# Two output column groups computed together with Strassen's method on half of the contraction

## The reference

```python
h = rmsnorm(x, norm_g)
q_a, k_a, v_a, g_a, u_p, g_p, q_m, g_m = split(h @ w_in)
y_a = moba_attention(q_a, k_a, v_a) * silu(g_a)                    # 8 heads x 128: 1024 wide
y_p = multiscale_pool(u_p, w_pool, pool_scale) * silu(g_p)         # 512 wide
y_m = memory_attention(q_m, *split(rmsnorm(mem) @ w_mem_kv)) * silu(g_m)   # 512 wide
y = concatenate([y_a, y_p, y_m]) @ w_out                           # (256 x 2048) @ (2048 x 2048)
return rmsnorm(x + y, final_norm_g)
```

## Time and profile before

| what | value |
|---|---|
| median of 3 runs | 437.32 us (437.22 to 437.8) |
| the profiled execution | 437.52 us |
| its span, first to last instruction | 435.4 us |
| mean granted TensorE clock | 0.997 of full speed |
| TensorE busy | 426.9 us (98%) |
| VectorE busy | 272.0 us (62%) |
| ScalarE busy | 223.1 us (51%) |
| POOL busy | 26.5 us (6%) |

### The profile page before, as it was taken

How to read it: one execution, slowest core, us unless ns; L and a number is a source line. 1 busy time by engine, 2 the same in 40 slices (tenths; PEclk the granted TensorE clock), 3 DMA queues, 4 the chain that set the end, 5 groups by cost and what they waited for, 6 DMA issues and landing times.

```text
span 435.4 us, 6073 instructions
## 1 busy us (share of the span) xinstructions
PE 426.9 (98%) x2276; PEld 367.7 (84%) x2276; DVE 272.0 (62%) x299; ACT 223.1 (51%) x303; POOL 26.5 (6%) x48
## 2 busy tenths in 40 slices
PE   9999999999999999999999999999999999999993
PEld 8888888888888888888988888888899888888882
DVE  4875865545464676746557677967668574648522
ACT  6864784743443435546544545455565545357311
POOL 1000000000000020000020200001000202120200
PEclk9999999999999999999999999999999999999998
DMA  8999959655556545542626556454645497756022
GB/s 284 403 401 411 402 202 383 188 186 191 183 184 190 193 159 176 177 139 100 213 98 199 188 190 192 152 192 172 215 145 191 137 401 237 213 174 193 0 98 97
DMA packets 25658, 89.78 MB, mean 206 GB/s; under 512 B 2976, under 2 KB 3232, under 8 KB 24736
## 3 DMA queue, kind: packets, MB, share of 16 engines
q1 hardware_dynamic: 24048, 81.16, 54.5%
q10 hardware_dynamic: 1584, 8.26, 4.8%
HBM read 87.31 MB, written 2.10 MB: 205 GB/s over the span
## 4 chain that ended last, share of the span: by engine, by line
PE 96%; issue 2%; DVE 0%; POOL 0%; ACT 0%; DVEq 0%; POOLq 0%
PE ps L405 35%; PE ps L408 17%; PE ps L421 11%; PE ps L423 11%; PE ps L422 11%; PE ps L386 3%; PE ps L393 1%; PE ps L503 1%; PE ps L458 1%; PE ps L494 1%; PE ps L473 1%; PE ps L495 0%; PE ps L457 0%; PE ps L469 0%; PE ps L563 0%
## 5 line engine op out<-in xcount | busy, mean ns | idle before, releaser
L770 DVE TENSOR_TENSOR w_lo<-w_raw,w_hi 128x1024 fp32r<-128x1024 f32 x137 | 173.9, 1282 | 107.8 <-ACT w_hi L580 107.5
L580 ACT ACTIVATE w_hi<-w_raw 128x1024 fp32r<-128x1024 f32 x137 | 143.6, 1058 | 124.6 <-PE ps L408 68.8
L405 PE MATMUL ps<-xT,w_hi 128*128 128x512 f32 x640 | 201.7, 396 | 0.0
L408 PEld LDWEIGHTS ps<-xT,w_lo 128*128 128x128 f32 x640 | 120.2, 188 | 28.4
L408 PE MATMUL ps<-xT,w_lo 128*128 128x256 f32 x640 | 125.8, 278 | 0.0
L405 PEld LDWEIGHTS ps<-xT,w_hi 128*128 128x128 f32 x640 | 97.8, 189 | 0.3
L421 PE MATMUL ps<-w_hi,yT 128*128 128x512 f32 x110 | 42.8, 389 | 0.0
L422 PE MATMUL ps<-w_lo,yT 128*128 128x512 f32 x110 | 42.8, 389 | 0.0
L423 PE MATMUL ps<-w_hi,yT 128*128 128x512 f32 x110 | 42.8, 389 | 0.0
L421 PE MATMUL ps<-w_hi,xT 128*128 128x512 f32 x64 | 25.4, 397 | 0.0
L423 PE MATMUL ps<-w_hi,xT 128*128 128x512 f32 x64 | 24.9, 390 | 0.0
(11 more groups left out here) (152 smaller groups left out, 399.6 us busy)
## 6 DMA issues: line engine op xcount, KB each, us to landing
w_raw<-in_w_in SPq DMA_DIRECT2D x96, 512.0 KB, 4.1
w_raw<-in_w_out SPq DMA_DIRECT2D x32, 512.0 KB, 4.2
w_raw<-in_w_mem_kv SPq DMA_DIRECT2D x13, 512.0 KB, 12.9
x_t_raw<-in_x_t SPq DMA_DIRECT2D x8, 256.0 KB, 13.3
rows<-in_x ACTq DMA_DIRECT2D x2, 1024.0 KB, 10.1
rows<-in_mem ACTq DMA_DIRECT2D x2, 1024.0 KB, 8.6
x_res<-in_x ACTq DMA_DIRECT2D x2, 1024.0 KB, 6.5
w_raw<-in_w_mem_kv SPq DMA_DIRECT2D x5, 256.0 KB, 5.4
```

Of the source, the lines that this page charges most:

```text
L405: pe.matmul(ps[:, bank0(g) + f, :], hi[:, t, f * P:(f + 1) * P], moving[:, kt], start=(kt == 0), stop=(kt == KT - 1), skip_group_check=True)
L408: m = pe.matmul(ps[:, bank0(g) + f, 0:S], lo[:, t, f * P:(f + 1) * P], moving[:, kt, 0], start=False, stop=(kt == KT - 1), skip_group_chec ...
L580: act.activation(halves_of(n)[0], w_raw[:, n % RAW], ACT.Copy).then_inc(hi_done, 1)
L770: dve.tensor_tensor(lo, w_raw[:, n % RAW], hi.bitcast(F32), ALU.subtract).then_inc(lo_done, 1)
```

## The change

Output groups 1 and 2 (`OUT1`, `OUT2`, 16 pieces) become one stretch of 22 units, 120 to 141. The contraction of branches 0 and 1 (8 of 16 tiles) is seen, for each branch, as a 2 x 2 block product: two halves of 128 tokens by two halves of the branch's four tiles, times those two halves by the two column groups. Seven block products with six matmuls each (`M1` to `M4`, `M6`, `N5`, `N7`) take the place of eight. The other two branches stay as they are (units `(OUT1, 4)` to `(OUT1, 7)` and the same of `OUT2`).

- Sums of weight blocks: f4 and f5 are each a plain load by SP and an adding DMA issued by POOL; f6 and f7 are sums by VectorE (`weight_sum`) at steps 118, 121, 124, 127. They are split into halves like a piece.
- Sums of `y` blocks: POOL makes four per branch right after VectorE has finished that branch (`block_sums`); ScalarE and VectorE split them in step 115.
- PSUM banks that hold a product needed in two results are copied once by ScalarE (four snapshots, `SNAPS`), and TensorE goes on adding into the bank. VectorE combines the snapshots with the residual (`combine`).
- SP's loop over the output groups is written out; it loads 14 pieces for the pair. The last group's split region shares memory with f5 to f7, so ScalarE waits for the low part of unit 141 before its first split there. `fg`, `squares` and some other buffers move in memory.

The diff, cut to its core:

```diff
-PIECES = GROUPS * PPG
+OUT1, OUT2 = OUT0 + 1, OUT0 + 2
+(M2, M3, M6, N5, M4, M1, N7) = range(GROUPS, GROUPS + 7)
+BRANCHES_MULTIPLIED = 2
+PAIR = OUT1 * PPG
+PAIR_UNITS = ((N5, 0), (M2, 0), (N5, 1), (M2, 1), (OUT1, 4), (M1, 0), (M3, 0), (OUT1, 5), (M1, 1), (M3, 1), (OUT1, 6),
+              (M4, 0), (M6, 0), (OUT1, 7), (M4, 1), (M6, 1), (OUT2, 4), (N7, 0), (OUT2, 5), (OUT2, 6), (N7, 1), (OUT2, 7))
+LAST_UNIT = PAIR + len(PAIR_UNITS)
+UNITS = LAST_UNIT + PPG
+LOADS = ((M2, 0), (M2, 1), (OUT1, 4), (M3, 0), (OUT1, 5), (M3, 1), (M6, 0), (M6, 1), (OUT1, 6), (OUT1, 7), (OUT2, 4),
+         (OUT2, 5), (OUT2, 6), (OUT2, 7)) + tuple((LAST, a) for a in range(PPG))
+F6, F7 = 1, 2
+SUM_STEPS = {OUT0 * PPG + 6: (F6, 0), PAIR + 1: (F6, 1), PAIR + 4: (F7, 0), PAIR + 7: (F7, 1)}
+SNAPS = {(M2, 1): 0, (N5, 1): 1, (M1, 1): 2, (M4, 1): 3}
+SNAPS_ORDER = (1, 0, 2, 3)
+OUT_BANK = {OUT0: 0, OUT1: 4, OUT2: 6, LAST: 0}
...
+        def unit(n):
+            if n < PAIR:
+                return divmod(n, PPG)
+            return PAIR_UNITS[n - PAIR] if n < LAST_UNIT else (LAST, n - LAST_UNIT)
+        def unit_of(g, a):
+            return LAST_UNIT + a if g == LAST else PAIR + PAIR_UNITS.index((g, a))
+        def piece_of(n):
+            if n < PAIR:
+                return n
+            return PAIR + LOADS.index(unit(n)) if unit(n) in LOADS else None
+        def slot(p):
+            return w_raw[:, p % RAW]
+        def whole_of(n):
+            if piece_of(n) is not None:
+                return slot(piece_of(n))
+            g, i = unit(n)
+            return f4[:, i] if g == N5 else f567[:, i, {M4: 0, M1: F6, N7: F7}[g]]
+        def sums_done(f, i):
+            return list(SUM_STEPS.values()).index((f, i)) + 1
...
-            if LAST * PPG <= n < LAST * PPG + SPLIT:
+            if LAST_UNIT <= n < LAST_UNIT + SPLIT:
                 return w_end[:, n % SPLIT, 0], w_end[:, n % SPLIT, 1]
             return w_hi[:, n % SPLIT], w_lo[:, n % SPLIT]
 
         def pieces_to_split(n):
 
 
-            ahead = n - (LAST * PPG - SPLIT)
+            ahead = n - (LAST_UNIT - SPLIT)
             if ahead < 0:
                 return range(n + SPLIT, n + SPLIT + 1)
-            return range(min(n + SPLIT + ahead, PIECES), min(n + SPLIT + ahead + 2, PIECES))
+            return range(min(n + SPLIT + ahead, UNITS), min(n + SPLIT + ahead + 2, UNITS))
...
-            with sp.Fori(0, GROUPS - OUT0) as g:
-                for a in range(PPG):
-                    sp.wait_ge(lo_done, g * PPG + ((OUT0 - 1) * PPG + a + 1))
-                    sp.dma_start(w_raw[:, a], out_w_dram[bass.ds(g, 1), a].rearrange("g p t c -> p (g t) c")
-                                 ).then_inc(landed[a], 16)
+            for a in range(PPG):
+                sp.wait_ge(lo_done, (OUT0 - 1) * PPG + a + 1)
+                sp.dma_start(w_raw[:, a], out_w_dram[0, a]).then_inc(landed[a], 16)
+            for r, (g, a) in enumerate(LOADS):
+                if r == 1:
+                    sp.wait_ge(probs_turned, 2 * len(JOBS))
+                    for i in range(BRANCHES_MULTIPLIED):
+                        sp.dma_start(f4[:, i], out_w_dram[OUT2 - OUT0, 2 * i]).then_inc(f4_landed[i], 16)
+                if r == 5:
+                    sp.wait_ge(piece_used, OUT0 * PPG)
+                    for i in range(BRANCHES_MULTIPLIED):
+                        sp.dma_start(f567[:, i, 0], out_w_dram[OUT1 - OUT0, 2 * i]).then_inc(f5_landed[i], 16)
+                if r < RAW:
+                    sp.wait_ge(lo_done, PAIR - RAW + r + 1)
+                else:
+                    past, i = LOADS[r - RAW]
+                    sp.wait_ge(lo_done, unit_of(past, i) + 1)
+                    if past == M6:
+                        sp.wait_ge(f67_done, sums_done(F6, i))
+                    if past == M3:
+                        sp.wait_ge(f67_done, sums_done(F7, i))
+                src = {M2: (OUT2, 2 * a), M3: (OUT2, 2 * a + 1), M6: (OUT1, 2 * a + 1)}.get(g, (g, a))
+                sp.dma_start(slot(PAIR + r), out_w_dram[src[0] - OUT0, src[1]]).then_inc(landed[(PAIR + r) % RAW], 16)
...
+            def block_sums(i):
+                s1, s2, s3, s4 = (s_raw[:, i, j] for j in range(4))
+                a11, a21 = gate[:, 0:TPP, 0:P], gate[:, 0:TPP, P:S]
+                a12, a22 = gate[:, TPP:NF, 0:P], gate[:, TPP:NF, P:S]
+                pool.wait_ge(y_ready, i + 1)
+                pool.tensor_tensor(s1, a21, a22, ALU.subtract).then_inc(s_step, 1)
+                pool.tensor_tensor(s3, a11, a21, ALU.subtract).then_inc(s_step, 1)
+                pool.wait_ge(s_step, 3 * i + 1)
+                pool.tensor_tensor(s2, s1, a11, ALU.subtract).then_inc(s_step, 1)
+                pool.wait_ge(s_step, 3 * i + 3)
+                pool.tensor_tensor(s4, a12, s2, ALU.add).then_inc(s_summed, 1)
             for i, g in enumerate(GATES):
+                if g == MEM_JOB:
+                    for k in range(BRANCHES_MULTIPLIED):
+                        pool.wait_ge(f4_landed[k], 16)
+                        pool.dma_start(f4[:, k], out_w_dram[OUT1 - OUT0, 2 * k], accum_op=ALU.add).then_inc(f4_summed[k], 16)
                 pool.wait_ge(gate_tanh, i + 1)
                 pool.wait_ge(att_ready, 2 * (i + 1))
                 pool.tensor_tensor(gate[:, :, :], gate[:, :, :], att[:, i % 2], ALU.mult).then_inc(gate_att, 1)
+                if i < BRANCHES_MULTIPLIED:
+                    block_sums(i)
+            for k in range(BRANCHES_MULTIPLIED):
+                pool.wait_ge(f5_landed[k], 16)
+                pool.dma_start(f567[:, k, 0], out_w_dram[OUT1 - OUT0, 2 * k + 1], accum_op=ALU.add).then_inc(f5_summed[k], 16)
...
+            def block_product(n):
+                hi, lo = halves_of(n)
+                g, i = unit(n)
+                first, second = slice(0, P), slice(P, S)
+                bank = {M2: bank0(OUT2) + 1, M1: bank0(OUT2) + 1, M4: bank0(OUT2) + 1, N7: bank0(OUT2) + 1,
+                        N5: bank0(OUT1), M6: bank0(OUT1), M3: bank0(OUT2)}[g]
+                for t in range(TPP):
+                    kt = NF * i + t
+                    left = {M2: (yT[:, kt, 0, first], yT[:, kt, 1, first]),
+                            M3: (yT[:, kt + TPP, 0, first], yT[:, kt + TPP, 1, first]),
+                            N7: (yT[:, kt + TPP, 0, second], yT[:, kt + TPP, 1, second]),
+                            N5: (s_hi[:, i, 0, t], s_lo[:, i, 0, t]), M1: (s_hi[:, i, 1, t], s_lo[:, i, 1, t]),
+                            M4: (s_hi[:, i, 2, t], s_lo[:, i, 2, t]), M6: (s_hi[:, i, 3, t], s_lo[:, i, 3, t])}[g]
+                    begun = not (i == 0 and t == 0 and g in (M2, N5, M3))
+                    pe.matmul(ps[:, bank, :], left[0], hi[:, t, :], start=not begun, stop=False, skip_group_check=True)
+                    pe.matmul(ps[:, bank, :], left[0], lo[:, t, :], start=False, stop=False, skip_group_check=True)
+                    m = pe.matmul(ps[:, bank, :], left[1], hi[:, t, :], start=False, stop=(t == TPP - 1), skip_group_check=True)
+                return m
...
-            for a in range(PPG - 1):
-                rows_are_tokens(LAST * PPG + a, yT, range(1, 2), KT - TPP - 1)
-            last_slices(LAST * PPG + PPG - 1, 1)
+            pe.wait_ge(evacuated, OUT0)
+            pe.wait_ge(s_split, 1)
+            for n in range(PAIR, LAST_UNIT):
+                g, a = unit(n)
+                if (g, a) == (M1, 0):
+                    pe.wait_ge(snapped, 1 + SNAPS_ORDER.index(SNAPS[M2, 1]))
+                if (g, a) == (OUT1, 4):
+                    pe.wait_ge(snapped, 1 + SNAPS_ORDER.index(SNAPS[N5, 1]))
+                if (g, a) == (M4, 0):
+                    pe.wait_ge(snapped, 1 + SNAPS_ORDER.index(SNAPS[M1, 1]))
+                if (g, a) == (OUT2, 4):
+                    pe.wait_ge(snapped, 1 + SNAPS_ORDER.index(SNAPS[M4, 1]))
+                pe.wait_ge(lo_done, n + 1)
+                (pair_piece if g < GROUPS else block_product)(n).then_inc(piece_used, 1)
+            pe.wait_ge(summed, 1)
+            for n in range(LAST_UNIT, UNITS):
+                pe.wait_ge(lo_done, n + 1)
+                m = rows_are_tokens(n, yT, range(0, 1))
+            m.then_inc(half_used, 1)
+            for n in range(LAST_UNIT, UNITS - 1):
+                rows_are_tokens(n, yT, range(1, 2), KT - TPP - 1)
+            last_slices(UNITS - 1, 1)
...
-                if SPLIT <= n < LAST * PPG:
+                if SPLIT <= n < LAST_UNIT:
                     act.wait_ge(piece_used, n - SPLIT + 1)
-                elif n == LAST * PPG:
-                    act.wait_ge(piece_used, OUT0 * PPG)
-                elif n >= LAST * PPG + SPLIT:
+                elif n == LAST_UNIT:
+                    act.wait_ge(lo_done, LAST_UNIT)
+                elif n >= LAST_UNIT + SPLIT:
                     act.wait_ge(piece_used, n - 2 * SPLIT + 1)
-                act.wait_ge(landed[n % RAW], 16 * (n // RAW + 1))
```

(86 more changed lines are left out.)

92 lines of the change are left out of this document (68 added, 24 removed).

## The result

The changed kernel takes 439.84 us, the median of 13 runs (437.15 to 441.47). The kernel before, run beside it, takes 437.45 us (13 runs, 437.21 to 437.8). The medians are 2.4 us apart. The ratio is 1.0046, with a 95% interval of 1.0032 to 1.0059: slower by 0.46%, or 2.0 us; it is smaller than the ratio of the medians (1.0055), as the means, 439.45 and 437.47 us, are also only 2.0 us apart. I had said 437.6 us, with 436.4 to 439.5 as the range. On the 437.32 us from which I set out the ratio makes 437.32 x 1.0046 = 439.3 us, just inside the upper end; the median itself is 0.3 us past it. Either way it lies outside what I had called the forecast case (436.9 to 438.2), and the likeliest outcome I had named, within 0.2%, did not come. The spread has itself grown, from 0.6 us to 4.3 us. The profiled execution took 439.23 us.

What follows compares the result with a forecast made beforehand. TensorE, busy 98%, was taken to bound the kernel. -2.72 + 2.5 + 0.4 = +0.2 us on the profiled 437.52 us gave 437.7; that execution lies 0.2 us over the median, so 437.6 us, range 436.4 to 439.5.

Steps and rivals of the forecast that it cites:

- forecast case: TensorE waits 2.2 to 3.5 us in all, giving 436.9 to 438.2 us; chance 0.56.
- What is removed: Output groups 1 and 2: 180 matmuls instead of 192, twelve fewer at 0.2267 us, -2.72 us.
- The start of the pair: Units 120 to 123 are short block products, so TensorE waits for unit 124's low part until 370.3: +2.5 us.
- the first obstacle: Unit 124's late low part; without it the first N5 snapshot on ScalarE would still cost 2.4 us.
- DMAs: Added plain loads (2 MB) and four adding DMAs, taken at 5 us each, cost nothing.
- 3 us to spare: Load of the first weight sum's second operand lands at 359.5; VectorE wants it at 362.6.
- Rival 3: First weight sum on VectorE waits for its load, landing at 364.5: +1.9 us, 439.5 us; chance 0.12.
- Rival 4: Clock falls to 1.2 GHz in TensorE's new gap; 3 us of it cost 1.5 us, 439.1 us; chance 0.03.
- The next three units: Splits on VectorE stretched beside POOL's weighting make TensorE wait at unit 126: +0.4 us.
- the rest: Later rounds of the pair hold, 0.5 to 0.7 us to spare at units 130 and 132: cost nothing.
- rival 2: VectorE slower than its undisturbed rows; waits of 3.6 or 4.7 us in all, 438.2 or 439.3 us; chance 0.17.
- What would show it: Signs: about 2.5 us wait before unit 124, below 1 us two units later, squares near 366.1, twelve fewer matmuls.

Runs made afterwards that it cites:

- both cures: Changed kernel with the squares of output group 0 four steps later and the second weight sum's plain loads three pieces later on SP: 435.23 us, ratio 0.9947.
- old pace of the products: Kernel with both cures, its four products with summed left operands reading plain activation blocks instead (another output): 434.9 us, one run.
- the loads in order: Changed kernel with the plain loads of the second weight sum's first operands three pieces later on SP: 438.48 us, ratio 1.0019.
- the dense filler: Kernel with the loads in order plus eight unused matmuls of 512 columns before the waits of unit 124: 437.62 us, ratio 1.0012.
- thin filler: Changed kernel plus six small unused matmuls of 128 columns before the waits of unit 124: 438.44 us, ratio 1.0036; profiled execution 437.58 us.
- second repetition: The changed kernel run and profiled once more, unaltered: 440.03 us, ratio 1.0069; profiled execution 439.17 us.

## Why the prediction was right in part and wrong in part

The time was 439.84 us; I had said 437.6. The direction was right, and the range was just wide enough, since it was drawn up to rivals 2 and 3. The sum was short by about 2 us, and so was the case I thought likeliest. (By its own terms the sum is 437.32 + 0.2 = 437.5; the 437.6 is a slip of 0.1 us.) Step by step:

**What is removed, -2.72 us: right.** 2264 matmuls issued, 12 fewer, and where nothing gets in the way they give their time back. With both cures the kernel is 2.1 us faster; at the old pace of the products (434.9 us, one run) 2.4 us.

**The start of the pair, +2.5 us: the mechanism right, to 0.1 us.** With the loads in order TensorE came to unit 124 at 370.44 for 370.3, and with the dense filler at 370.23. Moving the squares as well took the wait away. "Taking the first obstacle away alone would thus leave 2.4 us" was wrong, though: the snapshot kept TensorE back by nothing. I had put it behind the high parts of 124 and 125 as they were then timed, at 367.5 and 368.4; with the squares gone those move forward too, and with both cures the first snapshot runs at 366.73. A second obstacle must be timed with the first one gone.

**DMAs, nothing, "3 us to spare": this is the step that failed.** The load of the first weight sum landed at 364.1, where my sum of bytes had 359.5, and the 3 us to spare became a wait of 1.78 us in one profiled execution, 0.90 in another, 0 in a third. Two errors add up in the 4.6 us.

The first is the sum itself. It starts at 344.5, divides by 421 GB/s and puts this load last. Done for the kernel before, which has 1 MB less, it gives 344.5 + 5.2 MB / 421 GB/s = 357.0 for a load that landed at 359.6. The thin filler's profile, in which the residual and the norm gain were not delayed, has 362.1 for 359.5. Both times it is about 2.6 us short. I never tried the sum on the trace I had.

The second is the price of an adding DMA, 5 us, chosen "nearest to the plain load since the size is the same". It measured 9.3 us in the median, in the upper half of my own bounds of 4.2 to 11.4, and the longest, 11.6, lies outside them. The size is the same, but its packets take twice the engines' time per byte (5.6 against 2.9 us per MB); why, no run shows. I let that traffic only be early or late for itself ("even 11.4 us each end at 358.8"), which held: nothing waited for the first two adding DMAs. I did not let it push what stands behind it. In the changed kernel they still worked when the residual's loads were issued, the norm gain landed 2.7 us later than in the thin filler's profile (359.5 for 356.8), and the load of the sum 2.0 us later (364.1 for 362.1). With the second repetition in between (gain 358.4, load 363.0) the three profiles are in line. No run leaves the adding DMAs out, so this part rests on comparing profiles; and either error alone would have stayed within the 3 us.

**Rival 3**, which I gave 0.12, has that wait (+1.9 us reckoned, 1.6 to 1.8 measured, 1.4 between the medians), at that place and with that consequence. Its argument against, that the adding DMAs of the second sum wait for their own loads, is true: they were issued at 360.6 and 361.9, after those loads had landed. They did not have to overtake anything, since the landing times are later all along; whether they slowed the last 3.5 us of the load of the sum, beside which they ran, no run shows.

**Rival 4**, which I gave 0.03, is the second half. I priced a fall at 1.5 us, and a profiled one cost 1.2 to 1.3. But I took the 5 us of the earlier trace rows, of which a gap of 2.5 us "is half", as safety. That row is one case; it says nothing on how soon a fall can come, and three later profiles have it about 2 us after the last matmul. A pause of 3.0 us ended at the lower clock in one execution, one of 3.6 us did not in another, and of the twelve runs of a kernel whose profiled pause was 2.1 us seven had the lower mean clock. So it should have been about a coin toss on top of the forecast case, not a remote case beside it. The kernel with the loads in order shows it: its runs at a high clock lie at 437.1 to 437.9 us, its median at 438.48.

Together: 437.6 + 1.6 (the late load, by the timeline) + 0.75 (the clock) = 439.95, for 439.84 measured. That this meets the median so closely is partly luck: the wait for the load varied from 0 to 1.8 us, and the price of a fall is known from another kernel. The sum of the forecast was not far off for an execution in which neither occurs; the changed kernel has runs that look like it (437.15 to 437.42 us, at 0.994 and 0.995). I had treated rivals 3 and 4 as exclusive of each other and of the forecast, while both add to it.

**The next three units, +0.4 us, and the rest, nothing.** Unit 126 lost 0.3 us. Behind it TensorE's starts show no gap up to the last group, so rival 2, a slower VectorE, is not seen in the changed kernel. What I had missed is the pace: about 0.5 us, of which 0.3 are the products with summed left operands at 0.2333 instead of 0.2267 us. The other 0.2 us are 0.0015 us on each of the other matmuls, and no run explains them.

**What would show it.** "Squares near 366.1, high part near 367.5" failed by 1.6 us, which led straight to the weight sum. The wait at 124 with the low part as releaser was there, at 3.6 instead of 2.5 us. And the sign "in VectorE's queue before the first weight sum (the load)" was the one that came true.

## What to carry to other kernels

When an algebraic trick takes a few matmuls away from a kernel that TensorE bounds, look first at the chain of the engines that feed TensorE in the units that become short: here one operation in the wrong place on ScalarE was worth more than all the multiplications saved, and moving it turned +0.5% into -0.3%, or -0.5% with the loads reordered too. New traffic in a stretch where the DMA engines were idle is not free if a loaded stretch follows; add it to the backlog, not only to its own deadline. A sum of bytes that is to tell a landing time should first be tried on a load in the trace at hand. And a new pause on TensorE of the size seen here, 2 to 3.6 us, has to be priced with a fall of its clock, as an addition to every case in which the pause occurs.
